# A delta-rule scan on one core: six products with the state, then six with the new values

## The reference

```
def step(S, xs):
    q_i, k_i, u_i, w_i, g_i, a_i = xs
    v_new = u_i - jnp.einsum('bhck,bhkv->bhcv', w_i, S)
    o_i = (jnp.einsum('bhck,bhkv->bhcv', q_i * jnp.exp(g_i)[..., None], S)
           + jnp.einsum('bhij,bhjv->bhiv', a_i, v_new))
    g_last = g_i[..., -1:]
    S = (S * jnp.exp(g_last)[..., None]
         + jnp.einsum('bhck,bhcv->bhkv', k_i * jnp.exp(g_last - g_i)[..., None], v_new))
    return S, o_i
```

## Time and profile before

| | |
|---|---|
| median of 3 runs | 2641.05 us (2637.88 to 2643.32) |
| the profiled execution | 2638.55 us |
| its span in the trace | 2636.4 us |
| outside the span | 2.15 us |
| PE busy | 2543.8 us, 96% |
| DVE busy | 1718.5 us, 65% |
| ACT busy | 1226.5 us, 47% |
| PE on the chain that ended last | 84% |
| moved by DMA | 428.50 MB, mean 163 GB/s |

### The profile page before, as it was taken

One profiled execution on the slowest core, in us unless ns is written; L12 is line 12 of the kernel. 1 busy time (PEld: TensorE's weight loads), 2 busy tenths in 40 slices (PEclk: granted clock), 3 DMA queues, 4 the chain that ended last, 5 costly groups with the idle time before them and its releaser, 6 DMA issues.

```text
span 2636.4 us, 39407 instructions
## 1 busy us (share of the span) xinstructions
PE 2543.8 (96%) x17188; PEld 2337.9 (89%) x17188; DVE 1718.5 (65%) x1888; ACT 1226.5 (47%) x1275; POOL 0.2 (0%) x4
## 2 busy tenths in 40 slices
PE   7999999899998998999999999999899999999997
PEld 7998888789998978799999989987799999898876
DVE  5699855755888737565655657556656756577664
ACT  5544224554452225554334333337456556455573
POOL 0000000000000000000000000000000000000000
PEclk8999989999999979999999999999999999999999
DMA  5453222355442213455555555555445555545553
GB/s 209 166 178 129 96 79 89 136 192 180 175 175 95 86 61 112 165 204 179 186 183 191 178 190 188 183 201 199 159 176 176 179 189 176 185 180 179 183 193 119
DMA packets 63212, 428.50 MB, mean 163 GB/s; under 512 B 6976, under 2 KB 7104, under 8 KB 13504
## 3 DMA queue, kind: packets, MB, share of 16 engines
q1 hardware_dynamic: 60496, 414.97, 44.3%
q10 hardware_dynamic: 2544, 11.01, 1.1%
HBM read 421.76 MB, written 4.19 MB: 162 GB/s over the span
## 4 chain that ended last, share of the span: by engine, by line
PE 84%; DVE 6%; ACT 6%; issue 3%; DMA 0%; ACTq 0%; DVEq 0%; SPq 0%
PE PS L406 83%; ACT Q L878 2%; DVE Q L1456 2%; ACT WH L892 1%; DVE WL L1491 1%; PE PS L496 1%; DVE QA L1460 1%; ACT L878 1%; DVE Y L1456 1%; ACT QA L878 1%; DVE X L1460 1%; DVE Q L1460 0%; ACT HH L878 0%; PE PS L692 0%; DVE QA L1456 0%
## 5 line engine op out<-in xcount | busy, mean ns | idle before, releaser
L1491 DVE TENSOR_TENSOR WL<-W,WH 128x2048 fp32r<-128x2048 f32 (+2 forms) x388 | 861.2, 2224 | 544.1 <-ACT WH L892 544.0
L892 ACT ACTIVATE WH<-W 128x2048 fp32r<-128x2048 f32 (+2 forms) x388 | 717.5, 1858 | 779.8 <-PE PS L406 666.6
L406 PE MATMUL PS<-HH,WL 128*128 128x256 f32 x3392 | 564.2, 286 | 17.2 <-DVE WL L1491 12.1
L406 PE MATMUL PS<-HL,WH 128*128 128x256 f32 x3392 | 557.6, 284 | 0.0
L406 PE MATMUL PS<-HH,WH 128*128 128x256 f32 x3392 | 557.1, 284 | 0.0
L406 PEld LDWEIGHTS PS<-HH,WL 128*128 128x128 f32 x3392 | 474.0, 193 | 24.8 <-DVE WL L1491 12.7
L406 PEld LDWEIGHTS PS<-HL,WH 128*128 128x128 f32 x3392 | 473.3, 193 | 0.0
L406 PEld LDWEIGHTS PS<-HH,WH 128*128 128x128 f32 x3392 | 472.9, 193 | 0.0
L406 PE MATMUL PS<-WL,HH 128*128 128x512 f32 (+2 forms) x768 | 231.0, 382 | 10.0 <-DVE HL L1456 10.0
L406 PE MATMUL PS<-WH,HL 128*128 128x512 f32 (+2 forms) x768 | 223.7, 372 | 0.0
L406 PE MATMUL PS<-WH,HH 128*128 128x512 f32 (+2 forms) x768 | 222.7, 371 | 0.0
(11 more groups left out here) (135 smaller groups left out, 1990.1 us busy)
## 6 DMA issues: line engine op xcount, KB each, us to landing
W<-in_wall SPq DMA_DIRECT2D x378, 1024.0 KB, 4.8
W<-in_wall SPq DMA_DIRECT2D x16, 512.0 KB, 3.5
W<-in_wall SPq DMA_DIRECT2D x8, 536.0 KB, 3.4
X<-in_x SPq DMA_DIRECT2D x4, 512.0 KB, 7.4
X<-in_x ACTq DMA_DIRECT2D x1, 2048.0 KB, 10.2
xsave<-X ACTq DMA_DIRECT2D x1, 2048.0 KB, 10.7
X<-xsave ACTq DMA_DIRECT2D x1, 2048.0 KB, 11.0
Q<-in_g_post ACTq DMA_DIRECT2D x8, 256.0 KB, 3.3
```

The costliest lines, as they stand in the source:

```text
L406: return e.matmul(o, l, r, start=start, stop=stop, skip_group_check=True)
L892: e.activation(WH[:, s % NSPL, 0:m], W[:, c % NRAW, 0:m], ACT.Copy).then_inc(*up("hi", c))
L1491: e.tensor_tensor(WL[:, c % NRAW, 0:m], W[:, c % NRAW, 0:m], WH[:, s % NSPL, 0:m].bitcast(F32), ALU.subtract).then_inc(*up("lo", c))
```

## The change

The output's twelve products of a chunk are written as two loops over the heads. First come the six with the state, then the six with the new values. The products, their operands, their columns in PSUM, the flag `start` (true for the first product of the block alone), the waits and the signal after the last product are the same.

```diff
                     b = side(("dn", l, "o", c), ("dn_a", l, "o", c))
                     for h in range(6):
                         cs = slice(256 * h + 64 * c, 256 * h + 64 * c + 64)
-                        u0 = 256 * h + 128 * half + p0
                         mm(b[:, 64 * h:64 * h + 64], S[:, 128 * h:128 * h + 128], CQ[:, cs], start=(h == 0),
                            stop=False)
+                    for h in range(6):
+                        u0 = 256 * h + 128 * half + p0
                         i = mm(b[:, 64 * h:64 * h + 64], VN[p0:p0 + 64, 128 * h:128 * h + 128],
                                DI[p0:p0 + 64, u0:u0 + 64], start=False)
                     i.then_inc(*up("dn_p", l, "o", c))
```

## The result

The changed kernel takes 2614.96 us (median of 4 runs, 2611.31 to 2616.92), the one before 2639.47 in its 4 runs. The ratio is 0.9906, with a 95% interval of 0.9886 to 0.9926. The forecast was 2614. The profiled execution took 2615.06 us, its span is 2613.0, against 2638.55 and 2636.4: 23.4 us less in the span.

A forecast was written before the change was run, and what follows sets the result against it. PE was taken to bound the kernel, busy 96% of the span. Savings of 11.2 + 4.6 + 11.1 = 26.9 us gave 2614 us from the runs' median; range 2607 to 2620, and 2607 to 2629 with most of the second case.

The forecast's parts named there:

- Distance of the products: In eight blocks, ten of twelve products take 0.22 us instead of 0.36: 1.4 us a block, 11.2 us saved.
- The rule of the Trainium skill that spoke against the change: A load overlaps products under way only when its row group is another one; by it the saving would be 0.
- Half clock inside the blocks: Time that kv and blocks lose to the halved PE clock goes if the clock stays up: 4.6 us together.
- Half clock behind the blocks: Behind the first three blocks of both layers, 25.95 us at clock 0.50 would run at full clock: 11.1 us saved.
- a changed block looks like this or a little sparser: Likened a changed block to the projection of 268 columns, at clock 1.00 for 15 us, so the clock stays up.
- the rival: The clock falls all the same, as value products on half the rows could count for less; 2630 us, chance 0.12.
- Behind the last blocks: Behind the last block of each layer PE waits for ACT, as before; nothing was counted there.
- A clock that falls all the same: Only the distances count, 11.2 us: 2630 us, or 2622 if behind half the blocks; chance 0.12 for all or some.
- No change in pace: The short product itself, not the change of rows, costs 0.36 us, so nothing changes: 2641 us; chance 0.04.
- slower: In a run each product waits for the end of the one ahead, 0.43 us each: 2647 us; chance 0.02.
- swallowed gain: PE would reach unsplit weights, or ws before the state; 2628 us if half the gain went; chance 0.02.
- the slack at ws: Time between DVE's first state update in layer 0 and the next ws products needing it; 4.0 us forecast to remain.

The follow-up runs named there:

- the changed kernel again: The changed kernel with nothing altered, measured a second time beside other experiments: 2614.93 us, ratio 0.9909 to the kernel before.
- runs on 128 rows: Against the changed kernel: same order, state products then value products, but the value products use all 128 rows; 2607.33 us, ratio 0.9879.

## Why the prediction was right, and where it was off

*Distance of the products* (11.2 us): right. Each block is 1.40 us shorter at full clock, and the experiments show that the changes of rows cost it: 0.14 us for each change inside a block, whatever the order or the columns. (A lone block of the changed kernel has one of them, not the two that the prediction's last part counts.) What TensorE waits for at a change is not shown. The prediction took it for a load that can't begin while a product on other rows is under way. But in the last block of layer 0 before the change, the first load on 64 rows begins at 411.18 us, and the record of the product on 128 rows ahead of it goes on to 411.26:

```profile
410.98 0.28 PE L406 MATMUL PS<-Q 128*128 128x64 f32 x1
...
411.18 0.29 PEld L406 LDWEIGHTS PS<-Q 64*128 64x128 f32 x2
```

The ends of products are modelled in the profile, so this doesn't refute the reading either. The rule of the Trainium skill that spoke against the change (TensorE: Matmul & The Clock Gate, section The mechanism) fails here: loads on the same rows follow each other at 0.111 us under short products. What the trace shows is nearer the reverse: it is a change of rows that costs.

*Half clock inside the blocks* (4.6 us): right. 0.11 us of it is left, in one block.

*Half clock behind the blocks* (11.1 us): the mechanism is there, the size was wrong. In the profiled execution 13.4 of the 25.95 us stay, and by the factor of the earlier trace rows this term measured 0.43 x 12.55 = 5.4 us. The step that failed is "a changed block looks like this or a little sparser", set beside the projection of 268 columns, and the conclusion that the clock stays up. The whole scans show the same size, and also what the term is worth where it does stay up. Each window goes from the first kv product of a layer to the end of its last block. The four pairs are the kernel before, the changed kernel, the changed kernel again, and runs on 128 rows:

```profile
363.23:415.25 52.02, 51.14 (x285) 43.98 (x284) 19.24 (x35) 8.57 (x10) 0.00 (x0) 0.84 0.18 61
925.42:978.69 53.27, 52.39 (x285) 45.03 (x284) 19.22 (x35) 8.57 (x10) 0.00 (x0) 0.81 0.17 60
...
362.84:406.32 43.48, 42.60 (x285) 38.62 (x284) 19.22 (x35) 8.57 (x10) 0.00 (x0) 0.88 0.20 73
915.18:955.53 40.35, 39.48 (x285) 35.94 (x284) 19.23 (x35) 8.57 (x10) 0.00 (x0) 0.96 0.22 79
...
364.19:402.96 38.77, 37.89 (x285) 34.82 (x284) 19.24 (x35) 8.57 (x10) 0.00 (x0) 1.00 0.23 82
913.28:952.06 38.78, 37.90 (x285) 34.83 (x284) 19.23 (x35) 8.58 (x10) 0.00 (x0) 1.00 0.22 82
...
364.57:402.36 37.79, 36.91 (x285) 34.32 (x284) 19.23 (x35) 8.57 (x10) 0.00 (x0) 1.00 0.23 84
911.34:949.13 37.79, 36.91 (x285) 34.32 (x284) 19.23 (x35) 8.57 (x10) 0.00 (x0) 1.00 0.23 84
```

Both scans together took 105.3 us before and 83.8 after, 21.5 less. Without 11.2 for the distances and 4.5 inside the blocks, 5.8 are left for this term. In the second execution of the changed kernel they took 77.6 us, 27.7 less; without 11.2 and the full 4.6 this leaves 11.9: with the clock up behind all six blocks, the forecast's 11.1 us are there.

Why the clock fell is not settled. The projection of 268 columns uses all 128 rows in every product; half the block, and kv ahead of it, use 64. I had named this as what spoke for the rival and gave it too little. For it: with 128 rows in all of the block the kernel is 7.6 us faster than with the changed order alone, and in all four profiled executions of such kernels the clock is at 1.00 through both scans, in the changed kernel in one of two. Against taking it as shown: that one execution kept the clock with half the rows. And wider products also save time by themselves. With the clock at 1.00 in both, the scans take 77.6 us with the changed order and 75.6 on 128 rows. The 2.0 us are what 14 changes of rows cost at 0.14, eight inside the blocks and six between a block and the projection behind it. So of the 7.6 us, 2.0 are the rows' own price. The other 5.6 are likely the clock's for the most part, but no run separates the number of rows from the length of the stretch.

The mean granted clock of a whole execution is no witness here. It is 0.985 both in the execution of the changed kernel that lost the clock behind four blocks and in the one that lost it behind none, because it also falls elsewhere: where no block stands, for 13.65 us from 1872.43 us in the one and from 1867.79 us in the other.

*Behind the last blocks* (nothing counted): the clock came back sooner here too. The windows there, before in the first fence and after in the second:

```profile
415.40:425.00 9.60, 7.66 (x27) 4.66 (x28) 0.00 (x0) 6.76 (x8) 0.00 (x0) 0.64 0.01 2
975.40:990.00 14.60, 12.50 (x53) 8.83 (x53) 1.65 (x1) 8.55 (x9) 0.00 (x0) 0.65 0.00 1
```

```profile
406.50:417.00 10.50, 8.59 (x43) 6.27 (x44) 1.85 (x2) 8.63 (x9) 0.00 (x0) 0.84 0.01 2
955.60:970.00 14.40, 12.37 (x67) 9.67 (x68) 5.47 (x3) 11.67 (x10) 0.00 (x0) 0.88 0.06 16
```

A mean of 0.64 over 9.60 us is 2 x 0.36 x 9.60 = 6.9 us at half clock, and the window of layer 1 has 10.2; after, 3.4 and 3.5. That is 10.2 us less, but the window of layer 1 before begins inside the block, which ends at 978.69, and its first 3.3 us are those already counted as half clock inside. So 6.9 us are new, worth at most 0.43 x 6.9 = 3.0 us, since PE partly waits there. The starts of the same projection products behind the blocks, before in the first pair and after in the second, tell how much it was:

```profile
423.48 0.64 PE L406 MATMUL PS<-HH,WH 128*128 128x256 f32 x4
988.25 0.64 PE L406 MATMUL PS<-HH,WH 128*128 128x256 f32 x4
...
413.56 0.64 PE L406 MATMUL PS<-HH,WH 128*128 128x256 f32 x4
964.38 0.64 PE L406 MATMUL PS<-HH,WH 128*128 128x256 f32 x4
```

They come 9.92 and 23.87 us earlier, and the ends of the last blocks 8.93 and 23.16: 1.0 and 0.7 us were gained behind the blocks. So 11.2 + 4.5 + 5.8 + 1.7 gives 23.2 us, and the span shrank by 23.4.

The forecast of 2614 us was thus met in part by luck. Its sum was 26.9 us, 5.3 too much behind six blocks and 1.7 too little behind the last ones; the medians lie 24.5 us apart. And it was taken from the median of three runs, 2641.05, where the four runs beside the change have 2639.47. A saving 2.4 us too large from a start 1.6 us too high gives a forecast within 1 us of the 2614.96.

*The rivals.* A clock that falls all the same held in part, and not in every execution. Its 2622 us for half of the blocks were too much although the clock fell behind four of six: inside the blocks it stayed up, and where it fell behind one, it was for 3.4 us and not for 4.3. No change in pace, slower and swallowed gain did not occur: the slack at ws is 5.5 us where 4.0 were expected.

## What to carry to other kernels

Where small products on different sets of rows stand in turns, each change of rows costs time, here 0.14 us inside a block. Group them by rows, also with what stands ahead and behind, or, where the mask has zeros for the other rows anyway, use all rows for all: that freed the order and gained more. Look at the granted clock over such stretches, for a busy PE hides it. And compare stretch by stretch at the same clock before you explain the time of a whole kernel: here the clock alone moved two scans of the same program by 6.3 us.

## What was not expected of the hardware

The clock granted behind the same block of the same program was 0.51 in one execution and 1.00 in another: 2615.06 and 2610.82 us are the profiled executions of the two. Whether they ran on the same chip is not known. And value products widened from 64 rows to 128, of which half count for nothing, make the whole kernel 7.6 us faster, of which 2.0 us are changes of rows that go.
